# A hybrid decoder layer on one core: the sample states of the recurrence scaled on ScalarE at ticks of their own, and the keys of a head made ahead of other copies

## The reference

```
f = lb + (1.0 - lb) * jax.nn.sigmoid(rf)        # forget gate, (rows, 4 heads, 128)
kr = 1.0 - f                                    # keys
S_new = f[..., None] * S + kr[..., None] * i[..., None, :]     # for one new token
o = einsum('bhk,bhkv->bhv', q, S_new)
```

## Time and profile before

| | |
|---|---|
| median of 3 runs | 1227.35 us (1226.57 to 1230.59) |
| the profiled execution, its own time | 1227.49 us |
| its span in the trace | 1225.7 us |
| PE busy | 1201.1 us (98%) |
| DVE / ACT / POOL busy | 876.6 / 485.9 / 229.2 us |
| DMA | 169.8 MB, mean 139 GB/s |

### The profile page before, as it was taken

The page is one execution under the profiler, slowest core; times in us unless marked ns, Lnnn a source line. Parts: engine busy times, 40 slices in busy tenths (PEclk is TensorE's granted clock), DMA queues, the critical chain, the costliest instruction groups (busy, mean ns, idle before and its releaser), DMA issues.

```text
span 1225.7 us, 23606 instructions
## 1 busy us (share of the span) xinstructions
PE 1201.1 (98%) x9397; PEld 1186.5 (97%) x9397; DVE 876.6 (72%) x1525; ACT 485.9 (40%) x997; POOL 229.2 (19%) x162
## 2 busy tenths in 40 slices
PE   9999999999999999998999999999999999999997
PEld 9899999999998999998999999999999999999996
DVE  4877566573747685789877888888888575567676
ACT  6643543625140364455422322222222335455542
POOL 1000010101010000000023255657664220000011
PEclk9999999999998999999999999999999999999999
DMA  9431100105264442234355465867675376686466
GB/s 305 107 91 36 36 19 1 37 18 88 37 106 69 106 160 83 70 96 130 87 163 162 160 208 188 265 218 241 203 246 187 125 230 203 201 256 190 142 154 118
DMA packets 174014, 169.82 MB, mean 139 GB/s; under 512 B 23144, under 2 KB 126328, under 8 KB 173376
## 3 DMA queue, kind: packets, MB, share of 16 engines
q1 hardware_dynamic: 171728, 164.78, 45.4%
q0 software_dynamic: 2176, 3.52, 1.8%
HBM read 116.73 MB, written 52.58 MB: 138 GB/s over the span
## 4 chain that ended last, share of the span: by engine, by line
PE 61%; DVE 5%; issue 1%; ACT 0%; DVEq 0%; ACTq 0%
PE pair L1808 33%; PE pair L1848 18%; PE pair L1767 6%; PE pair L1548 3%; DVE mix L2289 1%; DVE mix L2314 1%; DVE w_lo L2247 1%; DVE qinv L2285 1%; PE pair L1739 0%; PE pair L1680 0%; PE pair L1750 0%; DVE act_lo L2297 0%; DVE mix L2452 0%; DVE acc L2351 0%; DVE mix L2272 0%
## 5 line engine op out<-in xcount | busy, mean ns | idle before, releaser
L1808 PE MATMUL pair<-act_hi,w_hi 128*128 128x258 f32 x704 | 199.6, 284 | 4.3 <-DVE w_lo L2247 2.7
L1808 PE MATMUL pair<-act_hi,w_lo 128*128 128x258 f32 x704 | 198.9, 283 | 0.0
L1808 PE MATMUL pair<-act_lo,w_hi 128*128 128x258 f32 x704 | 198.7, 282 | 0.0
L1848 PE MATMUL pair<-a_ring,w_hi 128*128 128x258 f32 x1056 | 189.6, 283 | 0.6 <-DVE mix L2452 0.5
L1548 PE MATMUL pair<-act_hi,w_hi 128*128 128x344 f32 x528 | 177.8, 337 | 0.2 <-DVE w_lo L1921 0.2
L1548 PE MATMUL pair<-act_hi,w_lo 128*128 128x344 f32 x528 | 170.0, 322 | 0.0
L1548 PE MATMUL pair<-act_lo,w_hi 128*128 128x344 f32 x528 | 169.7, 321 | 0.0
L1848 PEld LDWEIGHTS pair<-a_ring,w_hi 128*128 128x128 f32 x1056 | 162.5, 189 | 1.6 <-DVE mix L2452 0.9
L1808 PE MATMUL pair<-s_hi,w_lo 128*128 128x258 f32 x528 | 149.3, 283 | 0.0
L1808 PE MATMUL pair<-s_hi,w_hi 128*128 128x258 f32 x528 | 149.2, 283 | 0.0
L1808 PE MATMUL pair<-mix_r,w_hi 128*128 128x258 f32 x528 | 149.0, 282 | 0.0
(11 more groups left out here) (323 smaller groups left out, 2639.3 us busy)
## 6 DMA issues: line engine op xcount, KB each, us to landing
raw<-w_up_dram SPq DMA_DIRECT2D x26, 512.0 KB, 5.1
a_in<-h_sums SPq DMA_DIRECT2D x44, 258.0 KB, 3.4
rawx<-w_gate_dram SPq DMA_DIRECT2D x22, 512.0 KB, 4.8
w_quarter<-w_down_dram SPq DMA_DIRECT2D x44, 256.0 KB, 3.9
w_sums<-w_quarter SPq DMA_DIRECT2D x44, 256.0 KB, 4.6
rawx<-w_sums SPq DMA_DIRECT2D x44, 256.0 KB, 3.8
raw<-w_in_dram SPq DMA_DIRECT2D x18, 512.0 KB, 4.4
h_scratch<-mix SPq DMA_DIRECT2D x23, 258.0 KB, 2.1
```

The source lines that it names most:

```text
L1808: mm = pe.matmul(pair[psum_pair(n)][:, s, 0:QW], a[:, r, half + k, :], b, start=(k == 0 and i == 0), stop=(k == 3 and i == 2))
L1848: mm = pe.matmul(dpair(mt)[:, s, 0:a.shape[1]], b[:, cut], a, start=(m == 0 and n == 0), stop=(m == HALVES - 1 and n == 2))
```

## The change

The scaling of the sample states leaves POOL for ACT, as 8 instructions for each head (one for each sequence, with the gate as a scale for each partition). The steps get a table of ticks for each head: `r_scale` 97, 102, 106, 117; `r_sum` (the former `r_outer`) 98, 103, 108, 118; `r_o` 100, 104, 110, 120; the last two steps 122 and 124 in place of 123 and 125. SP's DMAs are placed relative to these ticks by the same rules as before. `key_rows` moves on ACT to the front of the recurrence steps of its tick, ahead of the copy `irow`; the small copy `f_s` moves from the gate into `key_rows`, behind `hk`, and those who waited for it (`prep` on POOL and DVE) wait for the gate itself.

```
-SR0, SRS = 99, 6
+R_SCALE, R_SUM, R_OUT, R_TURN = (97, 102, 106, 117), (98, 103, 108, 118), (100, 104, 110, 120), 122
...
-            d = tick - (SR0 + SRS * h)
-            out += [(s, h) for s, v in (("r_scale", 0), ("r_outer", 2), ("r_o", 4)) if d == v]
-        d = tick - (SR0 + SRS * NREC)
+            out += [(s, h) for s, v in (("r_scale", R_SCALE), ("r_sum", R_SUM), ("r_o", R_OUT)) if tick == v[h]]
+        d = tick - R_TURN
...
-                    pool.wait_ge(sem("f_done"), h + 1)
+                    pool.wait_ge(sem("f_gate"), 2 * CH * (h + 1))
...
-                if step[0] == "r_scale":
-                    h = step[1]
-                    pool.wait_ge(sem("st_in"), 16 * (h + 1))
-                    pool.wait_ge(sem("f_done"), h + 1)
-                    pool.tensor_tensor(st[:], st[:], bc(f_s[:, h, :].unsqueeze(2), [P, DECB, P]), ALU.mult).then_inc(sem("st_scaled"), 1)
...
-            if c == CH - 1:
-                act.wait_ge(sem("f_gate"), 2 * n + 2)
-                copy(f_s[:, m, :], r_f[:, SEQ:ROWS]).then_inc(sem("f_done"), 1)
...
+            act.wait_ge(sem("f_gate"), 2 * CH * (h + 1))
             act.activation(hk[:], r_f[:, 0:SEQ], ACT.Identity, scale=-1.0, bias=1.0).then_inc(sem("hk_prep"), 1)
+            copy(f_s[:, h, :], r_f[:, SEQ:ROWS]).then_inc(sem("f_done"), 1)
...
             for step in recurrence_steps(tick):
+                if step[0] == "prep":
+                    key_rows(step[1])
+            for step in recurrence_steps(tick):
...
-                if step[0] == "prep":
-                    key_rows(h)
...
+                if step[0] == "r_scale":
+                    h = step[1]
+                    act.wait_ge(sem("st_in"), 16 * (h + 1))
+                    act.wait_ge(sem("f_done"), h + 1)
+                    for b in range(DECB):
+                        ins = act.activation(st[:, b, :], st[:, b, :], ACT.Copy, scale=f_s[:, h, b:b + 1])
+                    ins.then_inc(sem("st_scaled"), 1)
...
-                if step[0] == "r_outer":
+                if step[0] == "r_sum":
```

More of the change, by code:

```diff
@@ L2013, in unit_read @@
                     dve.wait_ge(sem("ks_saved"), m)
+                    dve.wait_ge(sem("f_done"), m)
                     dve.wait_ge(sem("g_prod"), LEVELS * (m - 1) + 1)
@@ L2022, in unit_read @@
                     dve.wait_ge(sem("ks_saved"), NREC)
+                    dve.wait_ge(sem("f_done"), NREC)
                     dve.wait_ge(sem("g_prod"), LEVELS * (NREC - 1) + 1)
@@ L2124, in _ @@
                 if step[0] == "prep":
-                    dve.wait_ge(sem("f_done"), h + 1)
+                    dve.wait_ge(sem("f_gate"), 2 * CH * (h + 1))
                     if h:
```

## The result

The change takes 1233.7 us (median of 20 runs, 1229.7 to 1238.6) against 1229.1 us for the kernel before (20 runs on the same chip, 1224.8 to 1232.8): a ratio of 1.0036, interval 1.0023 to 1.0048. It is slower, by about as much as this measurement can just tell.

A forecast was written before the change was run, and what follows sets the result against it. PE, busy for 98% of the span, was taken to bound the kernel. From the profiled 1227.49 us, less 7.0, 0.96 and 0.3, plus 0.6, 6.1 and 3.1, came +1.5, so 1229.0 us; range 1223 to 1235.

The forecast's parts named there:

- likeliest case: Head 1's states and tile 19's weights both land late: 1229.0 us, span 1226.8 to 1231.5, chance 0.50.
- likeliest outcome: Whole kernel: time within 0.3% of the kernel before, chance 0.58.
- rival C: At `ot` and `diag` of head 3, a longer ACT chain makes the clock fall twice: about 1233.7 us, chance 0.22.
- Level 5 of head 3 (−7.0): Additions leave head 3's levels: PE's wait shrinks from 2.31 to 0.4, gaining 1.9 us plus 5.1 of lower clock.
- Keys first (−0.96, −0.3): Keys made ahead of `irow` on ACT: heads 0 and 1 gain 0.48 us each, head 3's old 0.3 wait goes.
- Head 0 (+0.6): PE reaches its step at tick 100 before DVE's additions end: a new wait of 0.6 us.
- Head 1 (+6.1): States land 13.4 us after issue at 343.0, so PE waits 6.1 us on the additions at tick 104.
- as after both shorter ones: Lower clock expected after head 1's 6 us wait, as after waits of 2.31 and 2.59 us; 3.1 us lost.
- rival B: Only tile 19's weights late; PE waits at unit 53, `ot`, `diag`: 1226.4 us, or 1229.8 with low clock; chance 0.15.
- Scaling at 1.6 us: Eight ACT instructions of 128 columns per head take 1.6 us, bounds 1.04 and 2.4.
- Later heads ... I cost these at nothing: Loads of heads 2 and 3 cost nothing, covered by ACT's slack of several us in each of ticks 109 to 117.
- Rival A: Head 1's states and tile 19's weights land in time: a gain of 7.2 us, 1220.3 us, chance 0.13.

The follow-up runs named there:

- first profile: The change itself, in the profiled execution that was the longest of its 20 runs: 1238.57 us.
- second execution: The change itself, unaltered, profiled a second time in a later measurement: 1229.37 us, beside 1231.44 for one run of the kernel before.

## Why the prediction was right or wrong

The median of 1233.7 lies in the range (1223 to 1235), but 4.7 us above the predicted time and above the likeliest case's own span (to 1231.5). Some 1.7 us of that is the kernel before, which took 1229.1 in 20 runs and not 1227.35; of a change forecast at +1.5 us, +4.6 came. The likeliest outcome, within 0.3%, did not come by the ratio of 1.0036, though its interval (1.0023 to 1.0048) reaches into it. What came is of rival C's kind, a clock that falls more than once, though not where and why C had it. C's condition was met (2.4 us of scaling in each head), but no wait of over 0.25 us stands at `ot` or `diag` of head 3. That its price of 1233.7 is the measured median to the digit is luck.

Against the profile of the kernel before, the terms that the prediction had came out in the first profile nearly as forecast: less 7.3 for the levels, less 1.0 for the keys, plus 0.4, 5.6 and 3.6 (the stretch at 357.70, in which PE worked 7.18 us at half), in all +1.3 us where +1.5 was forecast. The other 9.8 of its 11.1 us are what the sum lacked: 2.2 for the turn, 1.2 for the diagonal, 3.4 and 1.7 for the stretches at 385.00 and 323.65, and 1.3 in small items. So the sum came out as near the median as it did only because the median lost 4.6 us and not 11.1. Term by term:

- **Level 5 of head 3 (−7.0).** Right in mechanism: the wait of 2.31 and the stretch at half clock behind it are gone in every profile with the new ticks (what is left at level 5 is at most 0.91 us, with GpSimd scaling) and stayed with the keys alone.
- **Keys first (−0.96, −0.3).** Right: waits of about 0.55 for heads 0 and 1, and none over 0.2 for head 3 in the first profile. In the kernels where PE is not late from head 1 and the additions stand at 108 or 109, head 3's keys cost 0.9 to 1.1 (2.13 in the second execution): that small gain was cover by another loss.
- **Head 0 (+0.6).** 0.40.
- **Head 1 (+6.1).** In the first profile right nearly to the term: issue at 343.43 (343.0), landing after 12.4 us (13.4), a wait of 5.62, the clock at 0.50 from 357.7 (some 357 to 367). What failed is that it is always so. In the second execution the states landed after 5.4 us and only tile 19 was late, which is rival B's case. Its sum fails all the same: of its waits of 2.0, 2.9 and 1.7 us there is none at unit 53, 0.65 at `ot` and 2.13 at `diag`, as `w_hi` could start at 353.18 and not at 356.9. That B's 1229.8 stands near the 1229.37 measured is luck. The 20 times may be a mixture of cases that were priced as alternatives; two traces don't show it. The lower clock "as after both shorter ones" did come after the wait of 5.62; but it is no rule, as the second execution had none after 2.64 us.
- **Scaling at 1.6 us.** Mis-sized: 2.44, at the upper bound of 2.4. In the trace each of the eight takes 0.39 us and they start 0.29 to 0.30 apart. The 0.22 for 128 columns was drawn out from 512 and 1024 columns of another form, and is too short for this one by nearly half.
- **"Later heads ... I cost these at nothing".** This is the step that failed. Cover was named for ACT, in ticks 109 to 117, and none for DVE. At tick 108 the additions take 3.83 us beside POOL's products and hold the read of the diagonal (1.20 us and a stretch at 0.50, 6.85 us in the first profile, 3.4 in the kernels without the late load). The earlier trace rows had them at 2.19, alone; that at tick 108 they stand next to POOL's products was to be read from the order of the steps.
- **The turn at tick 122.** It has no term in the sum at all, and costs 2.2 us of waiting in both profiles of the change; given back, 2.8 us by the medians.
- **Rival A** (1220.3 with all transfers in time) was the profile's best case, and wrong in its sum: with the transfers in time the kernels stood at 1229, since the same two missing costs are in it. With all three put right it is 1222.4, or 6.7 us below the kernel before beside it, where A had a gain of 7.2; but that kernel also has head 2 scaled by POOL, so it is not A's. The Trainium skill says that descriptors of one queue start in order (page "DMA: Bandwidth & Descriptors", section "Two DMAs through the same engine are not ordered"). What I drew from it, that a load ahead of the small store would not suffer, agrees with the 4.0 us of the run with the weights early; the first profile's 12.4 us shows that being ahead is no safeguard.

On the neighbours of DVE the Trainium skill has a rule that I had not used: by "SBUF — State Buffer", section "Who interferes with whom", a Vector instruction with two inputs in SBUF contends with a GpSimd instruction that reads SBUF, and the later one blocks. The additions have two such inputs; 3.83 us beside the products and 2.19 at ticks 107, 109 and 106 agree with it in direction, and so does the first addition, which ended only with the POOL product that had started ahead of it. POOL's own products took the same 2.08 and 2.37 us in both cases.

What stays open: why a small store delays the load ahead of it in one execution and not in the next, and at one place of the queue and not at another; and how the low clock at 323.65, with so little waiting ahead of it, comes about. That stretch is not the change's alone: it stands near 324 in eight other traces, one of them at the old ticks, and not in the kernel before, the second execution, or two others.

## What to carry to other kernels

A step moved off one engine takes its wait along: on POOL a load late by some 8 us held nobody, on ACT it held the rest of the chain. When a table of ticks moves, price every row of it, the last ones too, and look at each new place for what stands behind on the same engine and what runs beside it on the neighbour. In a DMA queue look at where small scattered stores stand: a load with such a store close behind it can be late, and no order tried here was safe at every place. For head 1 it was enough to put the store behind both loads; at tick 98 the load just ahead of it was late in spite of that. And profile more than one execution, since the longest and the median can show different stories.

## What the runs showed of the hardware

- A store of 1024 pieces of 4 bytes (4 KB) took 10.2 us to land behind two loads, and where it stood between two loads of 512 KB these landed after 12.4 and 14.5 us (change), 10.0 and 11.8 (GpSimd scaling), or 5.4 and about 11 (second execution); with the store last, 4.4 and 5.6. With a third load of 512 KB just ahead of these and the store last, the load nearest the store took 10.3 to 14.1 us in eleven traces.
- Eight DVE additions of 128 columns: 2.18 or 2.19 us alone, 3.83 or 3.84 beside POOL's products; POOL's own took 2.08 and 2.37 us in both cases.
- ACT, 128 columns with a scale for each partition, SBUF to SBUF: 2.44 us for eight in a row (0.39 each, started 0.29 to 0.30 apart), where a plain copy of 1024 columns in one instruction takes 1.05.
- The clock fell to 0.50 after a wait of only 1.20 us too (385.0), for 3.4 us from between 376 and 379 in five other kernels after waits of 0.9 to 1.1 and 1.2, and at 323.65 with none of over 0.25 us since one of 0.69 at 316.13. After a wait of 2.64 us at 46.78 (second execution) it did not fall.
